# Trunk of a two-layer decoder: gate tiles finished one to two blocks later in three buffers, normalisation steps two blocks apart

## The reference

```
x  = layer_norm(ALPHA*x + o @ w_o, ...)          # "o" blocks
gu = x @ w_up ; g, u = gu[:, :2816], gu[:, 2816:] # "g" and "u" blocks
gc = conv_b + sum(conv_w[j] * shifted(g, j))      # causal, width 3
h  = silu(gc) * u
x  = layer_norm(ALPHA*x + h @ w_down, ...)        # "d" blocks
```

## Time and profile before

| | us |
|---|---|
| median of three timed runs | 3737.63 |
| lowest, highest | 3734.19, 3743.64 |
| the profiled execution, its own time | 3742.55 |
| span of that execution | 3740.8 |
| busy: PE, DVE, POOL, ACT | 3322.1, 1984.2, 1643.0, 1637.2 |
| mean granted TensorE clock | 0.948 |

### The profile page before, as it was taken

How to read it: one execution, slowest core, us unless ns; L and a number is a source line. 1 busy time by engine, 2 the same in 40 slices (tenths; PEclk the granted TensorE clock), 3 DMA queues, 4 the chain that set the end, 5 groups by cost and what they waited for, 6 DMA issues and landing times. The chain is left out here.

```text
span 3740.8 us, 58255 instructions
## 1 busy us (share of the span) xinstructions
PE 3322.1 (89%) x21128; PEld 3142.0 (84%) x21128; DVE 1984.2 (53%) x3669; ACT 1637.2 (44%) x3522; POOL 1643.0 (44%) x1452
## 2 busy tenths in 40 slices
PE   6999999999999958887999998959958889999997
PEld 6888888888888845877998998958848789999897
DVE  3344444344443421667557467437847673663773
ACT  3555454545455520444334344326734443443443
POOL 3434343434444410555546456433315554554562
PEclk9999999999999969999999999979979899999998
DMA  4672665367356528433443443311033234344352
GB/s 173 232 264 77 210 224 192 103 231 251 111 191 239 183 67 262 156 96 102 140 132 124 137 135 128 127 53 35 30 116 129 95 113 137 128 148 137 120 159 98
DMA packets 171495, 540.96 MB, mean 145 GB/s; under 512 B 40864, under 2 KB 89120, under 8 KB 168368
## 3 DMA queue, kind: packets, MB, share of 16 engines
q1 hardware_dynamic: 171200, 537.13, 43.2%
HBM read 497.21 MB, written 217.03 MB: 191 GB/s over the span
## 5 line engine op out<-in xcount | busy, mean ns | idle before, releaser
L101 PE MATMUL t_bank<-x_hi,t_w_hi 128*128 128x352 f32 (+1 forms) x2112 | 696.8, 330 | 61.2 <-DVE t_w_lo L1081 32.3
L1010 POOL TENSOR_TENSOR t_w_lo<-t_raw,t_w_hi 128x1024 fp32r<-128x1024 f32 (+1 forms) x228 | 552.4, 2423 | 368.1 <-ACT t_w_hi L892 365.2
L892 ACT CAST t_w_hi<-t_raw 128x1024 fp32r<-128x1024 f32 (+1 forms) x456 | 466.1, 1022 | 512.0 <-PE t_bank L103 510.9
L102 PE MATMUL t_bank<-x_lo,t_w_hi 128*128 128x352 f32 (+1 forms) x2112 | 685.9, 325 | 0.0
L103 PE MATMUL t_bank<-x_hi,t_w_lo 128*128 128x352 f32 (+1 forms) x2112 | 682.5, 323 | 0.0
L101 PE MATMUL a_gemm<-x_hi,a_w_hi 128*128 128x352 f32 (+1 forms) x1728 | 583.0, 337 | 29.2 <-DVE x_lo L486 29.2
L102 PE MATMUL a_gemm<-x_lo,a_w_hi 128*128 128x352 f32 (+1 forms) x1728 | 560.8, 325 | 0.0
L103 PE MATMUL a_gemm<-x_hi,a_w_lo 128*128 128x352 f32 (+1 forms) x1728 | 558.6, 323 | 0.0
L1081 DVE TENSOR_TENSOR t_w_lo<-t_raw,t_w_hi 128x1024 fp32r<-128x1024 f32 (+1 forms) x228 | 280.5, 1230 | 474.5 <-ACT t_w_hi L892 474.4
L101 PE MATMUL t_bank<-t_h_hi,t_w_hi 128*128 128x352 f32 (+1 forms) x1440 | 467.5, 325 | 37.0 <-DVE t_h_lo L1087 32.0
L101 PEld LDWEIGHTS t_bank<-x_hi,t_w_hi 128*128 128x128 f32 x2112 | 406.6, 193 | 74.0 <-DVE t_w_lo L1081 39.8
(11 more groups left out here) (211 smaller groups left out, 6142.4 us busy)
## 6 DMA issues: line engine op xcount, KB each, us to landing
t_raw<-w_up SPq DMA_DIRECT2D x264, 512.0 KB, 3.7
roll<-cache SPq DMA_DIRECT2D x128, 1023.5 KB
t_raw<-w_down SPq DMA_DIRECT2D x96, 512.0 KB, 3.7
a_raw<-w_a SPq DMA_DIRECT2D x72, 512.0 KB, 4.0
roll<-cache SPq DMA_DIRECT2D x16, 2044.0 KB
t_raw<-w_o SPq DMA_DIRECT2D x48, 512.0 KB, 3.8
t_raw<-w_down SPq DMA_DIRECT2D x48, 384.0 KB, 3.3
vT<-a_vt SPq DMA_DIRECT2D x24, 516.0 KB, 9.0
```

Of the source, the lines that this page charges most:

```text
L101: pe.matmul(out, w_hi, x_hi, start=first, stop=False)
L102: pe.matmul(out, w_hi, x_lo, start=False, stop=False)
L892: act.copy(w_hi[:, b % RING, cols], raw[:, b % RING, cols]).then_inc(s_whi, 1)
L1010: pool.tensor_tensor(w_lo[:, b % RING, cols], raw[:, b % RING, cols], f32(w_hi[:, b % RING, cols]), ALU.subtract).then_inc(s_wlo[0], 1)
```

## The change

Three things are changed in `trunk` and one in `norm_block`.

- SiLU of tile m-1 moves from the g block of tile m to its u block, behind `gate_rows`. The gate product of m-1 moves from the g block to the u block, behind `convolve(m)`. `high_h` and `low_h` of m-1 move from the u block of m to the g block of m+1. On POOL `low_h` there stands ahead of the weight split. At the end of the up loop `high_h` and `low_h` of tile 20 come in the first down block.
- `acc` has three buffers, by unit (22c + m) mod 3, and `convolve` waits for the low part of three tiles ago instead of two.
- `zt` has three buffers, by tile index mod 3; ACT waits for the residual of three tiles ago instead of four.
- Stages 1 and 2 are spaced two blocks per due time, from block 26 and block 50. The mean of stage 2 comes at block 36 instead of 31. Affine steps of stages 1 to 4 fall one block after the even block that they would have, so on u blocks.

```
@@ norm_block
-        return end + 2 + (5 if stage == 2 else 0)
-    if stage < NCH:
-        return (end + 2, 24, 38)[stage] + at
-    return end + 2 + 2 * at
+        return end + 2 + (10 if stage == 2 else 0)
+    if stage == 0:
+        return end + 2 + at
+    if what == "affine":
+        at += 0.5
+    return (26, 50)[stage - 1] + int(2 * at) if stage < NCH else end + 2 + int(2 * at)
@@ buffers
-        zt = sb("zt", [P, 4, CW])
+        zt = sb("zt", [P, 3, CW])
-        acc = sb("acc", [P, 2, CW])
+        acc = sb("acc", [P, 3, CW])
@@ evacuate_z (ACT)
-                need(act, s_zx, zi - 3)
+                need(act, s_zx, zi - 2)
@@ ACT, block by block
-                if kind == "g" and m > 0:
-                    silu(c, m - 1)
+                if kind == "g" and m > 1:
+                    high_h(c, m - 2)
                 if kind == "u":
                     gate_rows(b, c, m)
                     if m > 0:
-                        high_h(c, m - 1)
+                        silu(c, m - 1)
                 if kind == "d" and m == 0 and j == 0:
                     silu(c, FT - 1)
+                    high_h(c, FT - 2)
@@ POOL, block by block
                 kind, c, m, j = slots[b]
+                if kind == "g" and m > 1:
+                    low_h(c, m - 2)
+                if kind == "d" and m == 0 and j == 0:
+                    low_h(c, FT - 2)
                 if b % 2 == 0 and b + 2 < N_BLOCKS:
                     split(b + 2)
...
-                    if m > 0:
-                        low_h(c, m - 1)
@@ convolve (DVE)
-                need(dve, s_hlo, unit(c, m) - 1)
+                need(dve, s_hlo, unit(c, m) - 2)
@@ DVE, block by block
-                if kind == "g" and m > 0:
-                    gate(b, c, m - 1)
                 if kind == "u":
                     convolve(c, m)
+                    if m > 0:
+                        gate(b - 1, c, m - 1)
```

More of the change, by code:

```diff
@@ L903, in evacuate_z @@
                 need(act, s_blk, b)
-                need(act, s_zx, zi - 3)
+                need(act, s_zx, zi - 2)
                 if kind == "o":
-                    act.activation(zt[:, m % 4, 0:n], z_bank[m % 2][:, 0:n], ACT.Identity,
+                    act.activation(zt[:, zi % 3, 0:n], z_bank[m % 2][:, 0:n], ACT.Identity,
                                    bias=bias[:, m:m + 1]).then_inc(s_ze, 1)
                 else:
-                    act.copy(zt[:, m % 4, 0:n], z_bank[m % 2][:, 0:n]).then_inc(s_ze, 1)
+                    act.copy(zt[:, zi % 3, 0:n], z_bank[m % 2][:, 0:n]).then_inc(s_ze, 1)
             def silu(c, m):
@@ L913, in silu @@
                 act.wait_ge(s_conv, unit(c, m) + 1)
-                act.activation(acc[:, m % 2, 0:n], acc[:, m % 2, 0:n], ACT.Silu).then_inc(s_silu, 1)
+                act.activation(acc[:, unit(c, m) % 3, 0:n], acc[:, unit(c, m) % 3, 0:n], ACT.Silu).then_inc(s_silu, 1)
             def high_h(c, m):
@@ L918, in high_h @@
                 act.wait_ge(s_mul, unit(c, m) + 1)
-                act.copy(h_hi[:, m, 0:n], acc[:, m % 2, 0:n]).then_inc(s_hhi, 1)
+                act.copy(h_hi[:, m, 0:n], acc[:, unit(c, m) % 3, 0:n]).then_inc(s_hhi, 1)
             def gate_rows(b, c, m):
@@ L1029, in low_h @@
                 pool.wait_ge(s_hhi, unit(c, m) + 1)
-                pool.tensor_tensor(h_lo[:, m, 0:n], acc[:, m % 2, 0:n], f32(h_hi[:, m, 0:n]),
+                pool.tensor_tensor(h_lo[:, m, 0:n], acc[:, unit(c, m) % 3, 0:n], f32(h_hi[:, m, 0:n]),
                                    ALU.subtract).then_inc(s_hlo, 1)
@@ L1100, in residual @@
                 dve.scalar_tensor_tensor(out=dst, in0=f32(x_hi[:, m, off:off + n]), scalar=ALPHA,
-                                         in1=zt[:, m % 4, 0:n], op0=ALU.mult, op1=ALU.add).then_inc(s_zx, 1)
+                                         in1=zt[:, zi % 3, 0:n], op0=ALU.mult, op1=ALU.add).then_inc(s_zx, 1)
                 dve.wait_ge(s_zx, zi + 1)
@@ L1117, in convolve @@
                 k = n if c < NCH - 1 else n - NS
-                a = acc[:, mp, 0:k]
+                a = acc[:, unit(c, m) % 3, 0:k]
                 dve.wait_ge(s_gev, unit(c, m) + 1)
                 dve.wait_ge(s_hist, unit(c, m) + 1)
-                need(dve, s_hlo, unit(c, m) - 1)
+                need(dve, s_hlo, unit(c, m) - 2)
                 ins = dve.tensor_scalar(a, gbuf[:, mp, 0:k], tap(m, 0), tap(m, 3), ALU.mult, ALU.add)
                 if c == NCH - 1:
-                    ins = dve.scalar_tensor_tensor(out=acc[:, mp, k:n], in0=gbuf[:, mp, 2 + k:2 + n], scalar=tap(m, 2),
+                    ins = dve.scalar_tensor_tensor(out=acc[:, unit(c, m) % 3, k:n], in0=gbuf[:, mp, 2 + k:2 + n], scalar=tap(m, 2),
                                                    in1=state[:, m, 0, :], op0=ALU.mult, op1=ALU.add)
@@ L1133, in gate @@
             def gate(b, c, m):
-                n, mp = CHUNKS[c][1], m % 2
+                n, a = CHUNKS[c][1], acc[:, unit(c, m) % 3, :]
                 dve.wait_ge(s_blk, b)
                 dve.wait_ge(s_silu, unit(c, m) + 1)
-                dve.tensor_tensor(acc[:, mp, 0:n], acc[:, mp, 0:n], u_bank[mp][:, 0:n], ALU.mult).then_inc(s_mul, 1)
+                dve.tensor_tensor(a[:, 0:n], a[:, 0:n], u_bank[m % 2][:, 0:n], ALU.mult).then_inc(s_mul, 1)
             def center(stage, k):
```

## The result

Before 3738.82 us, after **3602.30 us** (medians of four runs each on one chip, 3595.86 to 3604.39 after); ratio 0.9632, 95% interval 0.9614 to 0.9649. That is 136.5 us less. The forecast was 84 us less (3653, range 3612 to 3705): the sign was right, the size wrong.

What follows compares the result with a forecast made beforehand. PE (89% busy) was taken as the bound, with 153.0 us excess in six up loops; 69.0 would remain, so 84 us gained (65 in chunk 0, 14 in chunk 1, 4 in chunk 2): 3653 us, range 3612 to 3705.

Steps and rivals of the forecast that it cites:

- Pot: Excess of the six up loops over PE's full pace of 169.5 or 157.6 us: 153.0 us in all.
- (a): Stages 1 and 2 at two blocks per step: in chunk 0 both 10 us waits for folded squares go.
- (b): Later SiLU, gate product, high_h, low_h: 9.86 us ring cut, new 7.6 us ring costs 9.7 per layer at 328 columns.
- (c): Norm steps in the up loops lengthen the new ring: 11.6 us per full stage, 3.1 without affine and low_x.
- ring P: Chain of waits through POOL's split, DVE's split, convolution, gate product, high_h, low_h; the forecast's new ring, put at 7.6 us.
- ring A: Not in forecast; chain through gate product, low_x, scale, x_hi, ACT's split, DVE's split, convolution: 8.40 us in a scaling pair.
- cushion: Slack per up loop before PE needs POOL's split: 2.8 us at 352 columns, 2.2 at 328.
- rival C: POOL's split behind low_h sets PE's pace; no gain at ring length r = 8.3, 3788 us at 8.7; chance 0.08.
- constant 49.6: Term in rival C's excess formula for the up loops: starts and norm steps less cushions, 49.6 us.
- (d): Three zt buffers, and low_h ahead of POOL's split in first down blocks: taken as 0; bounds 3 per layer, 3.4 us.
- A: Rival: only the spacing counts, the new ring is as slow as the old one: 3693 us; chance 0.11.
- B: Rival: everything hides, cushions and overlap absorb all but the two starts: 3588 us; chance 0.05.

Runs made afterwards that it cites:

- Run 1: The kernel before with only the new spacing of stages 1 and 2 (and affine steps on u blocks): 3711.82 us, ratio 0.9923.
- run 2: The kernel before with the order, `acc` and `zt` buffers of after, but the old `norm_block`: 3648.61 us, ratio 0.9759.
- run 5: The kernel after with one or two pads (extra POOL subtractions into a spare buffer, 0.9 us each) ahead of each low_h: 3691.80 and 3824.39 us.
- one-pad kernel: The kernel after with one extra POOL subtraction into a spare buffer ahead of each low_h: 3691.80 us, ratio 0.9867.

## Why the prediction was wrong in size

**Bound: right. Pot: right but for 10 us.** The stretches give 138.0 us back out of the 153.0 in which the prediction saw all of the gain. It took PE's pace from 1056 matmuls and put the matmuls of the mean and the variance at nothing; with the pace at 328 columns they are the 10 us above, which no order can win. The forecast took them for gain, which made its error smaller by luck.

**(a), the spacing: right.** PE's wait for the folded squares in the up loops is gone; chunk 0 is 172.6 us long (forecast 185). Run 1 shows what it does alone, run 2 what is left without it.

**(b), the new ring: the mechanism right, the size off by 0.3 to 0.4 us.** The ring exists and closes as written: the pads add their full length. It is 7.32 us at 352 columns (7.25 to 7.3 without an add in it) instead of 7.6. The surplus in the sum was 0.19 for POOL's two-column copy, which lies beside DVE's split, and 0.1 for the convolution (1.63, not 1.7). The sum took the rows of 352 columns for chunk 2 as well; at 328 the ring is 7.15 to 7.25 us (run 5), no longer than PE's own pair. The forecast had 0.44 over PE's pace there in each of 22 pairs, and these 9.7 us per layer are absent: 19.4 of the 54.0 us by which the forecast excess (69.0) was above the measured 15.0.

**(c), the failed step: "What the norm steps add to the new ring, in the order of the slots", 11.6 us for a full stage.** The steps were summed as if they all stood in ring P. DVE's stand in ring A, which in a centring pair is 0.6 us shorter than ring P, so that adds, fold and centre cost nothing where 3.1 us stood. In a scaling pair ring P grows only by what meets on the way: 0.65 for POOL's split waiting for scale (instead of 0.88 for low_x) and 0.51 for the convolution beside the affine steps (0.84 instead of 0.58 per step, instead of 1.25). And of the four pairs with affine steps only two have all of it: by the gate products of chunk 1 they are 8.23, 8.40, 8.42 and 7.84 us, for 9.73 each in the sum. They fall 2.1 us behind PE's 7.7 in all, and the cushion, put at 2.8, takes it (the sum's own terms, 7.7 less 4.98, make it 2.7). So PE never waits in chunk 1. By chunk the excess is 24.0 us under the forecast in chunk 0, 6.6 in chunk 1 and 23.4 in chunk 2; less the 19.4 of (b), the other 34.6 go to this step.

The pads test it once more. In the formula of rival C the part that the ring makes is 88 x 0.46 + 44 x 0.88, 79 us, with the pairs of the one-pad kernel (8.16 and 8.04). With the constant 49.6, which is the steps and the starts less the cushions, it gives 129; the loops show 88.6. The constant is 40 us too high: the ring and PE's own 10 us make the 88.6 alone.

"Scale and centre are beside low_h and cost nothing" was wrong for scale: it is shown with 1.62 instead of 0.88 and is part of ring A. It cost nothing on top because both rings are 8.4 us there, which is luck and no argument of the prediction.

The rule drawn on, that of two instructions asking for SBUF the later one is blocked for the whole of the other (the Trainium skill, SBUF — State Buffer, Who interferes with whom), holds in each case looked at: scale behind POOL's split 3.08 and 3.09, behind the rest of low_h 1.62. (The held step of the earlier trace rows ends 0.39 us after the POOL split beside it, at 1990.03 against 1989.64, and not with it as the prediction reads; it is held, and then does its own work.) The mistake was not the rule. It was to charge each hold to one ring, though an engine may be idle at that moment.

**(d): the bound about right, the value wrong.** The down blocks of chunk 0 are 3.2 and 3.7 us longer, in both layers with a wait of 2.5 us for POOL's low_h; the bound was 3.4, the value taken was 0. The argument "the split is wanted two blocks on" overlooked that stage 2's scale meets that split. In chunk 1 the down blocks are as before; those of chunk 2 are 2.4 and 4.6 us shorter, which wasn't forecast. Three `zt` buffers cost PE a wait of 1.1 and 1.0 us, within the bound of 3, and a fourth only moves it.

**Rivals.** A falls by runs 1 and 2: gate tiles alone bring 90. C falls: r is 7.3, not 8.3. Run 5 shows that one more instruction of 0.9 us in the ring takes two thirds of the gain, so C's sensitivity was real, though its constant was too high. B (3588) came nearest and was given 0.05; its counterargument, the sum of DVE's and POOL's work in a pair of 7.7 us, adds work that runs in parallel: such a pair is 8.4 us long, and only two pairs of a stage are full ones.

## What to carry to other kernels

Where engines wait for each other in turn, write down every ring that closes in a period, each with its own members; the period is the longest ring, and a step costs only by what it makes its own ring exceed the others. Test each ring on the chip with a pad of known length before adding terms to it: the pads gave 7.29 us at once. When two engines block each other, the order in which they ask matters more than the work: a POOL split that starts just before DVE's scale costs scale 2.2 us here, low_h put ahead of it costs it 0.7. And before a pot is called winnable, count in it the work that the bounding engine must do in any order.

## What the runs showed of the hardware

The scale step of 0.88 us is shown with 1.62 us behind the rest of POOL's low_h and with 3.08 and 3.09 behind its weight split (2.48 for the smaller form of 328 columns behind a smaller split), by what POOL had started before it. The hold also goes the other way: POOL's split of 2.40 us is shown with 3.06 when scale runs as it starts, and its two-column copy of 0.19 with 1.18 beside DVE's split. Beside the short affine steps a convolution step is shown with 0.84 us instead of 0.58: instructions of like length that alternate lose about 0.26 us each, far less than the 2.2 us that one long neighbour costs. Extra DVE steps of 0.88 us, put at the wrong place, cost 1.7 us each in the up loops (26.6 for sixteen).
